# Odd attention: the loads of a head in three groups, and the next unit's maxima and shift row earlier in the unit

## The chip, the cores and the metric

The kernel runs on one core of one Trainium2 chip. The metric is the device time of one execution in microseconds (us). The core has five engines that run their own instruction lists and meet by semaphores: TensorE (PE in the profile, with its weight loads as PEld), VectorE (DVE), ScalarE (ACT), GpSimd (POOL) and SyncE (SP), which here only issues DMAs. DMAs issued by SyncE, ScalarE and GpSimd run on 16 DMA engines.

## The reference, cut to what matters

The program is a two-layer diffusion backbone (1024 latent tokens, 256 context tokens, width 1024). The second, odd, layer has a two-dimensional neighbourhood attention of 8 heads with 64 channels: the latent tokens form 16 rows of 64, each query sees 8 rows x 16 columns around it with a position bias, and all 256 context tokens besides. In short:

```python
s_loc = einsum('bchd,bicjhd->bhcij', qr, kr) * scale + bias
s_ctx = einsum('bchd,bshd->bhcs', qr, k_ctx) * scale
p = softmax(concatenate([s_loc, s_ctx], axis=-1))
o = einsum(p_loc, vr) + einsum(p_ctx, v_ctx)
```

Around it stand the even layer, a gated convolution, projections, and in each layer a mixture of 16 experts of which every token takes two. They are not touched.

## The kernel before

The program is a row of phases with a barrier of all engines at the end of each. `attend_odd` is one of them; the phases before it leave q and k (each split into a high and a low part), v and the bias tables in device memory. After it `output_odd` multiplies by the output weights.

**Units and steps.** `OddPlan` writes the order of all work into one list of events, and each engine walks through that same list and takes its own part of each event. A unit u = 2h + g is one half (g = 0 or 1, 512 queries) of head h; there are 16. A unit has 8 steps, each one block of 128 keys: two of context and six of local keys. The local ones reach only part of the 512 queries: 384, 512, 512, 512, 256, 128 columns for g = 0 and 128, 256, 512, 512, 512, 384 for g = 1. The order is context, three local, context, three local.

**One step.** `scores`: TensorE makes q times k in two products into `ps_s` (L1966 with kb and qb, L1967 with k1 and qr, whose row 64 carries minus the query's maximum, the "shift row"). For local keys VectorE adds the bias table edgeT or innerT (L1913). ScalarE takes the exponential into `pT` (L1801). `values`: TensorE multiplies by vo into `ps_o` (L1976). Scores run two steps ahead of values; `ps_s` has two buffers and `pT` three.

**Maxima and shift.** The softmax needs a maximum per query. Four `max` events of the next unit, one for each 128 queries, make q times k again, with the queries as rows (L1941 and L1942, or L1945 to L1947, into `ps_t`), and VectorE adds the table edge or inner and takes the maximum (L1889 and L1891, or L1893). After the fourth, one reduction writes minus the maxima into nmx (L1900, semaphore nmx_done). `shift`: TensorE transposes nmx in four products (L1952), and ScalarE copies the result into row 64 of qr (L1806). The first scores of a unit wait for that copy. `max` and `shift` share the two `ps_t` buffers in turn. Before the change the maxima of unit u+1 stand in steps 0 to 3 of unit u and the shift in step 6.

**The rest of a unit.** `drain`: ScalarE copies sums and totals out of `ps_o` and, after the second half of a head, issues the load of vo for head h+2 (L1818). After an odd head, VectorE inverts the sums in four reciprocals (`invert`, L1918, steps 2 to 5 of the next unit), GpSimd multiplies (L1853), ScalarE rounds the result (`normal`, L1823, step 6, ahead of the shift), GpSimd makes the low part (L1856). `weights`: in steps 3 and 7 of units 0 to 7 ScalarE rounds a piece of the output weights (L398) out of one of two buffers, GpSimd makes its low part (L1841) and issues the next load into that buffer (L1829).

**Loads.** Each head has 13 loads: qb twice and kb twice (L1778), inner twice and edge (L1769, L1770), qr (L1780), k1 (L1781), innerT twice and edgeT (L1769, L1770), all by SyncE, and vo by ScalarE. Heads h and h+2 share buffers. SyncE issues head h's loads when the last values product of head h-2 is through, and all 13 count on one semaphore, `head_in`. Three consumers wait for its full count: TensorE and VectorE at the first maximum of a head, ScalarE at the shift.

Of the kernel before, what the change touches and what calls it, by code (L numbers as in the profile page):

```python
# [31 lines left out]
P = 128  # L32
# [5 lines left out]
HD = 64  # L38
GRID_W = 64
# [78 lines left out]
def as_f32(ap):  # L118
    return ap.bitcast(F32)
# [1529 lines left out]
class OddPlan:  # L1649
# [3 lines left out]
    def __init__(self):  # L1653
        self.units = [(h, g) for h in range(8) for g in range(2)]
        self.steps, self.first, self.last = [], {}, {}
        for u, (h, g) in enumerate(self.units):
            self.first[u] = len(self.steps)
            local = self.local(g)
            self.steps += [(u, LT, 0, 4)] + local[:3] + [(u, LT + 1, 0, 4)] + local[3:]
            self.steps[self.first[u]:] = [(u, *s[1:]) for s in self.steps[self.first[u]:]]  # L1660
            self.last[u] = len(self.steps) - 1
        self.events, self.banks = [], {}
        self.next_bank, self.uses = 0, [0, 0]
        self.added, n = {}, 0
        for s, (u, kt, c0, c1) in enumerate(self.steps):
            if kt < LT:
                n += 1
            self.added[s] = n
        for j in range(4):
            self.event('max', 0, j)  # L1670
        self.event('shift', 0)
        for s in range(2):
            self.event('scores', s)
        nu = len(self.units)
        for u in range(nu):
            for s in range(self.first[u], self.last[u] + 1):
                at = s - self.first[u]
                if u + 1 < nu and at < 4:
                    self.event('max', u + 1, at)
                if u and self.units[u - 1][0] % 2:  # L1680
                    if 2 <= at < 6:
                        self.event('invert', u - 1, at - 2)
                    if at == 6:
                        self.event('normal', u - 1)
                if u + 1 < nu and at == 6:
                    self.event('shift', u + 1)
                if s % 4 == 3 and s // 4 < 16:
                    self.event('weights', s // 4)
                if s + 2 < len(self.steps):
                    self.event('scores', s + 2)  # L1690
                self.event('values', s)
            self.event('drain', u)
        for c in range(4):
            self.event('invert', nu - 1, c)
        self.event('normal', nu - 1)
# [22 lines left out]
def attend_odd(nc, k, w):  # L1718
# [2 lines left out]

    plan = OddPlan()
    units, steps = plan.units, plan.steps
    LOADS = 13
    with Phase(nc, "at1") as ph:
        kb, k1 = ([ph.sb(f"{n}{p}", [P, NT * P], F32R) for p in range(2)] for n in ("kb", "k1"))
        qb, qr = ([ph.sb(f"{n}{p}", [P, SEQ], F32R) for p in range(2)] for n in ("qb", "qr"))
# [13 lines left out]
        ps_s = [ph.ps(f"ps_s{i}", [P, 512]) for i in range(2)]  # L1741
        ps_o = [ph.ps(f"ps_o{i}", [P, 512]) for i in range(2)]
        S = {n: ph.sem(n) for n in ("filled filled_pool nmx_done shifted scored added exp_done valued drained inverted a_ready a_hi a_lo").split()}
        head_in = [ph.sem(f"head_in{p}") for p in range(2)]
        t_full = [ph.sem(f"t_full{i}") for i in range(2)]
        t_read = [ph.sem(f"t_read{i}") for i in range(2)]

# [5 lines left out]
        def emptied(eng, what, *x):  # L1753
            b, n = plan.banks[(what, *x)]
            eng.wait_ge(t_read[b], n + 1)

        def head_ready(eng, h):
            eng.wait_ge(head_in[h % 2], 16 * LOADS * (h // 2 + 1))

        with nc.Block() as block:  # L1760

            @block.sync
            def _(sp):
                def tables(h, o, edges, inners, first):

                    p = h % 2
                    for half in range(2):
                        s, a = slice(half * GRID_W, (half + 1) * GRID_W), (first + half) * GRID_W
                        sp.dma_start(inners[p][s, a:a + 8 * GRID_W], k.inner_d[o, h, s, :]).then_inc(head_in[p], 16)  # L1769
                    sp.dma_start(edges[p][:, :, :], k.edge_d[o, h]).then_inc(head_in[p], 16)  # L1770

                for h in range(8):
                    p = h % 2
                    if h >= 2:
                        sp.wait_ge(S["valued"], plan.last[2 * (h - 2) + 1] + 1)
                    r = slice(h * HD, (h + 1) * HD)
                    for dst, src in ((qb[p][0:HD, :], k.qh_d), (qb[p][HD:P, :], k.qh_d), (kb[p][0:HD, :], k.kh_d), (kb[p][HD:P, :], k.kl_d)):
                        sp.dma_start(as_f32(dst), src[r, :]).then_inc(head_in[p], 16)  # L1778
                    tables(h, 0, edge, inner, 0)
                    sp.dma_start(as_f32(qr[p][0:HD, :]), k.ql_d[r, :]).then_inc(head_in[p], 16)  # L1780
                    sp.dma_start(as_f32(k1[p][0:HD, :]), k.kh_d[r, :]).then_inc(head_in[p], 16)  # L1781
                    tables(h, 1, edgeT, innerT, 1)

            @block.scalar
            def _(act):
                for h in range(2):
                    act.dma_start(vo[h][:, :, h, :], k.v_d.rearrange("(t p) (h d) -> h p t d", p=P, d=HD)[h]).then_inc(head_in[h], 16)
                for ev in plan.events:
                    what, i = ev[0], ev[1]
                    if what == 'scores':  # L1790
# [11 lines left out]
                    elif what == 'shift':  # L1802
                        h, g = units[i]
                        ps, read = full(act, *ev)
                        head_ready(act, h)
                        nc.scalar.activation(qr[h % 2][HD:HD + 1, g * 512:(g + 1) * 512], ps[0:1, 0:512], ACT.Copy).then_inc(read, 1)  # L1806
                    elif what == 'weights':
                        w.round_hi(act, i, i + 1)
                    elif what == 'drain':
# [6 lines left out]
                        nc.scalar.activation(total[own, g, :], ps_o[g][own, :], ACT.Copy).then_inc(S["drained"], 1)  # L1816
                        if g == 1 and h + 2 < 8:
                            act.dma_start(vo[h % 2][:, :, h % 2, :], k.v_d.rearrange("(t p) (h d) -> h p t d", p=P, d=HD)[h + 2]  # L1818
                                          ).then_inc(head_in[h % 2], 16)
                    elif what == 'normal':  # L1820
                        h, g = units[i]
                        act.wait_ge(S["a_ready"], h // 2 * 2 + g + 1)
# [36 lines left out]
            def _(dve):  # L1859
# [15 lines left out]
                for ev in plan.events:  # L1875
                    what, i = ev[0], ev[1]
                    if what == 'max':
                        (h, g), j = units[i], ev[2]
                        p = h % 2
                        if j == 0:  # L1880
                            head_ready(dve, h)
                        ps, read = full(dve, *ev)
                        if i:
                            dve.wait_ge(S["nmx_done"], i)
# [16 lines left out]
                    elif what == 'scores':  # L1901
# [7 lines left out]
                        if m > 2:  # L1909
                            before = max(x for x in range(s) if plan.added[x] == m - 2 and steps[x][1] < LT)  # L1910
                            dve.wait_ge(S["exp_done"], before + 1)
                        dve.wait_ge(S["scored"], s + 1)
                        nc.vector.tensor_tensor(sb[(m - 1) % 2][:, 0:n], ps_s[s % 2][:, 0:n], tab[:, slot * GRID_W:slot * GRID_W + n], ALU.add  # L1913
                                                ).then_inc(S["added"], 1)
# [6 lines left out]
            def _(pe):  # L1921
# [8 lines left out]
                for ev in plan.events:  # L1930
                    what, i = ev[0], ev[1]
                    if what == 'max':
                        (h, g), j = units[i], ev[2]
                        p, tile = h % 2, 4 * g + j
                        if j == 0:
                            head_ready(pe, h)
                        ps, done = bank(*ev)
                        q = qb[p][:, tile * P:(tile + 1) * P]
                        ctx = kb[p][:, LT * P:NT * P]
# [14 lines left out]
                    elif what == 'scores':  # L1954
# [2 lines left out]
                        p, n = h % 2, (c1 - c0) * P  # L1957
                        if s == plan.first[u]:
                            emptied(pe, 'shift', u)
                        if s >= 2:  # L1960
                            if steps[s - 2][1] < LT:
                                pe.wait_ge(S["added"], plan.added[s - 2])
                            else:
                                pe.wait_ge(S["exp_done"], s - 1)
# [937 lines left out]
```

## Time and profile before

| what | us |
|---|---|
| median of 3 runs (lowest to highest) | 3387.43 (3386.11 to 3391.88) |
| the profiled execution | 3392.86 |
| its span in the trace | 3391.1 |
| first load of odd attention issued | 2339.0 |
| first maximum | 2361.60 |
| first scores of unit 0, of unit 15 | 2369.37, 2629.27 |
| granted TensorE clock, mean over the span | 0.868 |

Busy shares of the whole span are TensorE 76%, VectorE 46%, ScalarE 30%, GpSimd 18%. They are means over all phases; odd attention is some 300 us of the 3391. A row of a timeline has start, duration, engine, line, what is written from what, and in square brackets the idle time before it and what ended it. In the rows by stretch (rows 1) the columns are: the stretch and its length, busy time (with the number of instructions) of TensorE, its weight loads, VectorE, ScalarE and GpSimd, then the granted clock (1.00 is 2.4 GHz), the busy share of the DMA engines, and GB/s. Starts of DMA issues are marked SPq; landing times are from issue to the last byte's semaphore.

### The profile page before, as it was taken

How to read it: one execution, taken by the hardware profiler on the slowest of the kernel's cores; microseconds unless marked ns; L12 is line 12 of the kernel's file. 1: busy time of each engine (PE TensorE's matmuls, PEld its weight loads, DVE VectorE, ACT ScalarE, POOL GpSimd, SP SyncE). 2: the span in 40 equal slices, each digit the busy share in tenths (PEclk: the TensorE clock that was granted, in tenths of full speed). 3: DMA queues.
4: the chain of work that ended last, by engine and by line, in shares of the span. 5: the costliest groups of instructions: out<-in, count | busy, mean ns of one | idle time of the engine just before them, and what ended most of it. 6: DMA issues, size and time to landing. Idle time of an engine off the chain costs nothing. (4 is left out here: it accounts for less than half of the span.)

```text
span 3391.1 us, 31818 instructions
## 1 busy us (share of the span) xinstructions
PE 2580.9 (76%) x10767; PEld 1873.4 (55%) x10768; DVE 1563.3 (46%) x2166; ACT 1008.9 (30%) x1326; POOL 602.7 (18%) x560
## 2 busy tenths in 40 slices
PE   5499788898954999997337974785777792999990
PEld 0388555565633888885026532664444571788780
DVE  2255543433333566563532862333455223566754
ACT  1122242332312445442111012211433111455640
POOL 0233122111112000000121600231210332000001
PEclk9999798897966999998568987897888885999995
DMA  9111344101046777663920513666544224768856
GB/s 385 53 42 38 94 172 147 56 29 56 28 169 180 258 284 269 215 234 142 403 69 19 149 38 85 165 151 164 125 105 93 94 93 146 260 246 329 305 196 216
DMA packets 304556, 534.56 MB, mean 158 GB/s; under 512 B 126157, under 2 KB 150203, under 8 KB 298300
## 3 DMA queue, kind: packets, MB, share of 16 engines
q1 hardware_dynamic: 228848, 387.56, 34.5%
q0 software_dynamic: 25520, 85.58, 7.4%
q10 hardware_dynamic: 50076, 59.99, 5.1%
q8 instruction: 63, 1.03, 0.1%
q14 instruction: 49, 0.40, 0.0%
HBM read 431.72 MB, written 116.03 MB: 162 GB/s over the span
## 5 line engine op out<-in xcount | busy, mean ns | idle before, releaser
L2548 DVE TENSOR_TENSOR ex_gu_lo<-mw_gu,ex_gu_hi 128x2048 fp32r<-128x2048 f32 x128 | 287.3, 2287 | 78.8 <-ACT ex_gu_hi L2468 78.5
L2468 ACT ACTIVATE ex_gu_hi<-mw_gu 128x2048 fp32r<-128x2048 f32 x128 | 237.5, 1911 | 120.9 <-DVE ex_y L2595 114.8
L1611 PE MATMUL at_ps_o<-at_pT,at_v_one 128*128 128x512 f32 x336 | 187.8, 642 | 1.7 <-ACT at_pT L1391 1.7
L2626 PE MATMUL ex_ps_g<-ex_gu_hi,ex_xT_hi 128*128 128x512 f32 x408 | 169.6, 416 | 8.1 <-issue 4.9
L2626 PE MATMUL ex_ps_y<-ex_d_hi,ex_hT_hi 128*128 128x512 f32 x408 | 166.7, 409 | 9.1 <-DVE ex_d_lo L2548 7.7
L1391 ACT ACTIVATE at_pT<-at_ps_s 128x512 f32<-128x512 f32 x168 | 99.5, 595 | 232.6 <-PE at_ps_s L1604 232.3
L2548 DVE TENSOR_TENSOR ex_d_lo<-mw_d,ex_d_hi 128x2048 fp32r<-128x2048 f32 x64 | 143.8, 2288 | 53.4 <-ACT ex_d_hi L2468 53.4
L2626 PE MATMUL ex_ps_g<-ex_gu_lo,ex_xT_hi 128*128 128x512 f32 x408 | 164.7, 404 | 0.0
L2626 PE MATMUL ex_ps_g<-ex_gu_hi,ex_xT_lo 128*128 128x512 f32 x408 | 164.3, 403 | 0.0
L2626 PE MATMUL ex_ps_y<-ex_d_hi,ex_hT_lo 128*128 128x512 f32 x408 | 162.0, 397 | 0.0
L2626 PE MATMUL ex_ps_y<-ex_d_lo,ex_hT_hi 128*128 128x512 f32 x408 | 162.0, 397 | 0.0
L2626 PE MATMUL ex_ps_u<-ex_gu_hi,ex_xT_lo 128*128 128x512 f32 x408 | 161.2, 395 | 0.0
L2626 PE MATMUL ex_ps_u<-ex_gu_lo,ex_xT_hi 128*128 128x512 f32 x408 | 161.2, 395 | 0.0
L2626 PE MATMUL ex_ps_u<-ex_gu_hi,ex_xT_hi 128*128 128x512 f32 x408 | 161.2, 395 | 0.0
L2443 POOL TENSOR_TENSOR ex_at<-ex_slots,ex_nil 128x1 int32<-128x1 int32 x53 | 16.4, 310 | 804.6 <-PE ex_ps_x L2620 799.9
L1584 PE MATMUL at_ps_t<-k_both,at_q_both 128*128 128x512 f32 (+1 forms) x208 | 111.5, 576 | 54.6 <-DVE at_mx L1501 37.7
L1501 DVE TENSOR_REDUCE at_mx<-at_ps_t 128x1 f32<-128x512 f32 (+1 forms) x208 | 115.6, 582 | 46.3 <-PE at_ps_t L1584 45.0
L2468 ACT ACTIVATE ex_d_hi<-mw_d 128x2048 fp32r<-128x2048 f32 x64 | 119.1, 1908 | 28.5 <-DVE ex_y L2570 19.8
L1976 PE MATMUL at_ps_o<-at_pT,at_vo 128*128 128x512 f32 (+3 forms) x256 | 123.3, 566 | 2.9 <-ACT at_pT L1801 2.5
L865 DVE SCALAR_TENSOR_TENSOR pc_acc<-pc_yT,pc_taps,pc_acc 128x512 f32<-128x512 f32 x120 | 112.4, 1011 | 0.0
L1584 PEld LDWEIGHTS at_ps_t<-k_both,at_q_both 128*128 128x128 f32 x208 | 44.3, 213 | 116.8 <-DVE at_mx L1501 71.7
L2468 ACT ACTIVATE ex_xT_hi<-ex_ps_x 128x512 fp32r<-128x512 f32 x106 | 57.8, 596 | 171.4 <-PE ex_ps_x L2620 171.4
(486 smaller groups left out, 6130.6 us busy)
## 6 DMA issues: line engine op xcount, KB each, us to landing
mw_gu<-in_moe_w_gate SPq DMA_DIRECT2D x32, 2048.0 KB, 10.9
mw_gu<-in_moe_w_up SPq DMA_DIRECT2D x32, 2048.0 KB, 15.8
mw_d<-in_moe_w_down SPq DMA_DIRECT2D x32, 2048.0 KB, 7.7
y_d<-ex_y ACTq DMA_DIRECT2D x51, 512.0 KB
mod_mod_w<-in_ada_w SPq DMA_DIRECT2D x24, 1024.0 KB, 11.1
y_d<-at_zero POOLq DMA_DIRECT2D x36, 512.0 KB, 5.2
co_mod_w<-in_ada_w SPq DMA_DIRECT2D x16, 1024.0 KB, 14.1
edge_d<-rows_d SPq DMA_DIRECT2D x64, 160.0 KB, 3.3
```

The costliest lines, as they stand in the source:

```text
L865: ins = nc.vector.scalar_tensor_tensor(acc[q][:, c, :], src, taps[:, c, t:t + 1], acc[q][:, c, :], ALU.mult, ALU.add)
L1391: nc.scalar.activation(pT[u % 3][:, :], ps_s[u % 3][:, :], ACT.Exp).then_inc(S["exp_done"], 1)
L1501: nc.vector.tensor_reduce(mx[:, hd, c:c + 1], ps[:, :, :].rearrange("p c t -> p (c t)")[:, 0:runs[c][1]], AX.X, ALU.max).then_inc(read, 1)
L1584: nc.tensor.matmul(ps[:, :, :].rearrange("p c t -> p (c t)")[:, 0:n], q_both[i % 2][g][:, j * P:(j + 1) * P], k.k0_both[:, g, a:a + n], st ...
L1611: nc.tensor.matmul(ps_o[g][:, :], v_one[:, kt, g:g + 2, :].rearrange("p a d -> p (a d)"), pT[u % 3][:, :], start=(u == plan.first[i, g]), ...
L1976: nc.tensor.matmul(ps_o[g][:, c0 * P:c1 * P], vo[h % 2][:, kt, :, :].rearrange("p a d -> p (a d)"), pT[s % 3][:, 0:n], start=(s == plan.fi ...
L2443: nc.gpsimd.tensor_tensor(at[:, :], slots[:, bass.ds(within(n, most), 1)], nil[:, :], ALU.add).then_inc(S["at_ready"], 1)
L2468: nc.scalar.activation(dst, src, ACT.Copy).then_inc(sem, 1)
L2548: sub = lambda dst, a, b, sem: nc.vector.tensor_tensor(dst, a, as_f32(b), ALU.subtract).then_inc(sem, 1)
L2626: mm = nc.tensor.matmul(out, a[:, c, :], b[:, c, cols], start=(c == 0 and j == 0), stop=(c == chunks - 1 and j == 2))
```

## The change

The 13 loads of a head count on three semaphores: `bias_in` (3: inner twice, edge), `qk_in` (4: qb twice, kb twice) and `rest_in` (6: qr, k1, innerT twice, edgeT, vo). SyncE issues them in that order, and each group waits for what frees its own buffers in head h-2: the bias group for the last maxima, the qk and rest groups for the last scores, innerT and edgeT for the last add. VectorE's first maximum waits for `bias_in`, TensorE's for `qk_in`; the first scores product of a unit and VectorE's adds of a head's first half wait for `rest_in`; ScalarE's shift waits for no load any more. In the plan the four maxima of the next unit stand in steps 0, 0, 1 and 2, and the shift in step 4.

```diff
-                if u + 1 < nu and at < 4:
-                    self.event('max', u + 1, at)
+                for j in [j for j, turn in enumerate((0, 0, 1, 2)) if u + 1 < nu and turn == at]:
+                    self.event('max', u + 1, j)
...
-                if u + 1 < nu and at == 6:
+                if u + 1 < nu and at == 4:
                     self.event('shift', u + 1)
...
-        def head_ready(eng, h):
-            eng.wait_ge(head_in[h % 2], 16 * LOADS * (h // 2 + 1))
+        def bias_ready(eng, h):
+            eng.wait_ge(bias_in[h % 2], 16 * 3 * (h // 2 + 1))
+        def qk_ready(eng, h):
+            eng.wait_ge(qk_in[h % 2], 16 * 4 * (h // 2 + 1))
+        def rest_ready(eng, h):
+            eng.wait_ge(rest_in[h % 2], 16 * 6 * (h // 2 + 1))
...
                 for h in range(8):
                     p = h % 2
                     if h >= 2:
-                        sp.wait_ge(S["valued"], plan.last[2 * (h - 2) + 1] + 1)
+                        sp.wait_ge(S["nmx_done"], 2 * (h - 2) + 2)
+                    tables(h, 0, edge, inner, 0, bias_in)
+                    if h >= 2:
+                        sp.wait_ge(S["scored"], plan.last[2 * (h - 2) + 1] + 1)
                     r = slice(h * HD, (h + 1) * HD)
                     for dst, src in ((qb[p][0:HD, :], k.qh_d), (qb[p][HD:P, :], k.qh_d), (kb[p][0:HD, :], k.kh_d), (kb[p][HD:P, :], k.kl_d)):
-                        sp.dma_start(as_f32(dst), src[r, :]).then_inc(head_in[p], 16)
-                    tables(h, 0, edge, inner, 0)
-                    sp.dma_start(as_f32(qr[p][0:HD, :]), k.ql_d[r, :]).then_inc(head_in[p], 16)
-                    sp.dma_start(as_f32(k1[p][0:HD, :]), k.kh_d[r, :]).then_inc(head_in[p], 16)
-                    tables(h, 1, edgeT, innerT, 1)
+                        sp.dma_start(as_f32(dst), src[r, :]).then_inc(qk_in[p], 16)
+                    sp.dma_start(as_f32(qr[p][0:HD, :]), k.ql_d[r, :]).then_inc(rest_in[p], 16)
+                    sp.dma_start(as_f32(k1[p][0:HD, :]), k.kh_d[r, :]).then_inc(rest_in[p], 16)
+                    if h >= 2:
+                        sp.wait_ge(S["added"], plan.added[plan.last[2 * (h - 2) + 1]])
+                    tables(h, 1, edgeT, innerT, 1, rest_in)
...
                     elif what == 'shift':
-                        head_ready(act, h)
...
                         if j == 0:
-                            head_ready(dve, h)
+                            bias_ready(dve, h)
...
+                        if g == 0:
+                            rest_ready(dve, h)
                         dve.wait_ge(S["scored"], s + 1)
...
                         if j == 0:
-                            head_ready(pe, h)
+                            qk_ready(pe, h)
...
                         if s == plan.first[u]:
                             emptied(pe, 'shift', u)
+                            rest_ready(pe, h)
```

## Rows read from the trace of the kernel before

**Rows 1.** Busy time by stretch in odd attention (columns below).

```profile
2382.80:2393.90 11.10, 10.46 (x46) 7.21 (x46) 7.24 (x17) 6.89 (x13) 3.67 (x4) 1.00 0.14 47
2393.90:2407.00 13.10, 12.14 (x46) 7.60 (x46) 7.35 (x17) 6.92 (x13) 3.66 (x4) 1.00 0.76 157
2407.00:2418.00 11.00, 1.66 (x9) 1.32 (x9) 0.29 (x1) 2.49 (x5) 1.81 (x2) 0.68 0.90 245
2432.75:2448.50 15.75, 12.42 (x47) 7.61 (x47) 10.34 (x21) 7.77 (x14) 6.26 (x7) 1.00 0.80 164
2509.90:2527.20 17.30, 14.01 (x46) 8.54 (x46) 10.35 (x21) 7.25 (x13) 3.76 (x4) 0.89 0.72 168
```

**Rows 2.** The list of waits over odd attention: total, times, longest us.

```profile
PE at_ps_t L1941 <- DMA at_edgeT<-edge_d: 67.6, 7, 30.2
...
PE at_ps_s L1966 <- ACT at_qr L1806: 21.5, 16, 2.6
```

**Rows 3.** TensorE's timeline: first product of a unit's maxima (start, duration us).

```profile
2361.60 0.76 PE L1941 MATMUL at_ps_t<-at_kb,at_qb 128*128 128x512 f32 x1 [30.23 <-DMA at_edgeT<-edge_d]
...
2384.16 0.48 PE L1941 MATMUL at_ps_t<-at_kb,at_qb 128*128 128x512 f32 x1
...
2396.06 0.69 PE L1945 MATMUL at_ps_t<-at_kb,at_qb 128*128 128x512 f32 x1
...
2417.96 0.79 PE L1941 MATMUL at_ps_t<-at_kb,at_qb 128*128 128x512 f32 x1 [9.32 <-DMA at_edgeT<-edge_d]
...
2434.89 0.69 PE L1945 MATMUL at_ps_t<-at_kb,at_qb 128*128 128x512 f32 x1
...
2457.50 0.80 PE L1941 MATMUL at_ps_t<-at_kb,at_qb 128*128 128x512 f32 x1 [6.09 <-DMA at_edgeT<-edge_d]
...
2471.53 0.69 PE L1945 MATMUL at_ps_t<-at_kb,at_qb 128*128 128x512 f32 x1
...
2513.63 0.69 PE L1945 MATMUL at_ps_t<-at_kb,at_qb 128*128 128x512 f32 x1
```

**Rows 4.** TensorE's timeline: first scores product of units 0, 1, 4, 8, 15.

```profile
2369.37 0.79 PE L1966 MATMUL at_ps_s<-at_qb,at_kb 128*128 128x512 f32 x1 [0.67 <-ACT at_qr L1806]
...
2382.79 0.50 PE L1966 MATMUL at_ps_s<-at_qb,at_kb 128*128 128x512 f32 x1 [0.67 <-ACT at_qr L1806]
...
2432.75 0.50 PE L1966 MATMUL at_ps_s<-at_qb,at_kb 128*128 128x512 f32 x1 [2.59 <-ACT at_qr L1806]
...
2509.88 0.80 PE L1966 MATMUL at_ps_s<-at_qb,at_kb 128*128 128x512 f32 x1 [2.59 <-ACT at_qr L1806]
...
2629.27 0.50 PE L1966 MATMUL at_ps_s<-at_qb,at_kb 128*128 128x512 f32 x1 [0.67 <-ACT at_qr L1806]
```

**Rows 5.** Groups by line over odd attention.

```profile
L1893 DVE CUSTOM_DVE_ANT_0 at_junk<-at_ps_t,at_inner 128x896 f32<-128x896 f32 x32 | 34.5, 1084 | 6.8 <-PE at_ps_t L1947 6.6
...
L1918 DVE RECIPROCAL at_sums<-at_sums 128x128 f32<-128x128 f32 x32 | 29.6, 936 | 2.9 <-ACT at_total L1816 2.9
```

**Rows 6.** Timeline of one step: an add on VectorE and its values product.

```profile
2390.22 0.69 DVE L1913 TENSOR_TENSOR at_sb<-at_ps_s,at_edgeT 128x512 f32<-128x512 f32 x1
...
2391.69 1.13 PE L1976 MATMUL at_ps_o<-at_pT,at_vo 128*128 128x512 f32 x2
```

**Rows 7.** SyncE's issues, and us from issue to landing by stretch.

```profile
2342.81 0.59 SPq L1770 DMA_DIRECT2D at_edge<-edge_d  x1
...
at_edge<-edge_d SPq DMA_DIRECT2D x1, 640.0 KB, 12.5
...
ow_w_raw<-in_od_w_out POOLq DMA_DIRECT2D x2, 256.0 KB, 9.2
...
2435.37 1.08 SPq L1778 DMA_DIRECT2D at_qb<-qh_d  x2
...
2437.14 0.60 SPq L1778 DMA_DIRECT2D at_kb<-kl_d  x1
...
at_kb<-kl_d SPq DMA_DIRECT2D x1, 320.0 KB, 9.5
```

More of the change, by code:

```diff
@@ L1723, in attend_odd @@
     units, steps = plan.units, plan.steps
-    LOADS = 13
     with Phase(nc, "at1") as ph:
@@ L1743, in attend_odd @@
         S = {n: ph.sem(n) for n in ("filled filled_pool nmx_done shifted scored added exp_done valued drained inverted a_ready a_hi a_lo").split()}
-        head_in = [ph.sem(f"head_in{p}") for p in range(2)]
+        bias_in, qk_in, rest_in = ([ph.sem(f"{n}{p}") for p in range(2)] for n in ("bias_in", "qk_in", "rest_in"))
         t_full = [ph.sem(f"t_full{i}") for i in range(2)]
@@ L1763, in _, with tables @@
             def _(sp):
-                def tables(h, o, edges, inners, first):
+                def tables(h, o, edges, inners, first, sem):
                     p = h % 2
@@ L1768, in tables @@
                         s, a = slice(half * GRID_W, (half + 1) * GRID_W), (first + half) * GRID_W
-                        sp.dma_start(inners[p][s, a:a + 8 * GRID_W], k.inner_d[o, h, s, :]).then_inc(head_in[p], 16)
-                    sp.dma_start(edges[p][:, :, :], k.edge_d[o, h]).then_inc(head_in[p], 16)
+                        sp.dma_start(inners[p][s, a:a + 8 * GRID_W], k.inner_d[o, h, s, :]).then_inc(sem[p], 16)
+                    sp.dma_start(edges[p][:, :, :], k.edge_d[o, h]).then_inc(sem[p], 16)
                 for h in range(8):
@@ L1786, in _ @@
                 for h in range(2):
-                    act.dma_start(vo[h][:, :, h, :], k.v_d.rearrange("(t p) (h d) -> h p t d", p=P, d=HD)[h]).then_inc(head_in[h], 16)
+                    act.dma_start(vo[h][:, :, h, :], k.v_d.rearrange("(t p) (h d) -> h p t d", p=P, d=HD)[h]).then_inc(rest_in[h], 16)
                 for ev in plan.events:
@@ L1818, in _ @@
                             act.dma_start(vo[h % 2][:, :, h % 2, :], k.v_d.rearrange("(t p) (h d) -> h p t d", p=P, d=HD)[h + 2]
-                                          ).then_inc(head_in[h % 2], 16)
+                                          ).then_inc(rest_in[h % 2], 16)
                     elif what == 'normal':
```

## The prediction

> **What bounds the kernel now.** The kernel is one long sequence of stages with a barrier after each, and the diff touches one of them, odd attention. So I read first the busy time in stretches of that stage, then its list of waits, then TensorE's own timeline at the first product of each unit, then SyncE's issues and their landing times. The stage starts at 2339 us (the first load of head 0 at SyncE) and ends near 2640 us. A unit is half a head's queries (g is 0 or 1), eight steps long; sixteen of them follow each other, u = 2h + g.
>
> In the stretches [rows 1] TensorE is close to full between 2382.8 and 2407.0 (10.46 busy in 11.10 us, 12.14 in 13.10), at granted clock 1.00, which is 2.4 GHz. Then comes a stretch of 11.00 us with 1.66 us of TensorE's work while the DMA engines are at 0.90 and the clock falls to 0.68. The waits [rows 2] name it: seven times TensorE waits for the load into edgeT in front of L1941, 67.6 us in all. The first is the start of the stage (30.23), the other six, 37.4 us together, lie at the first maximum of heads 2 to 7 ([rows 3] has two of the six: 9.32 and 6.09). All 13 loads of a head count on one semaphore, edgeT is the last of them, and they are issued only once the last product of head h-2 is through. The second wait, 21.5 us in 16 times, is the first score product of each unit for the shift row that ScalarE copies [rows 2]. It comes in two sizes [rows 4]: 0.67 us, and 2.59 us where ScalarE's `normal` copy stands ahead of it in the same step and waits for GpSimd, which waits for the fourth reciprocal.
>
> **What a step costs.** TensorE takes a scores product of 512 columns in two matmuls and its values product in two slower ones; at 2.4 GHz I count two clocks a column for scores and four for values, 0.43 and 0.85 us (the pair of values at 2391.69 is shown with 1.13 us, its end overlapping what follows [rows 6]). With the 3328 columns of a unit, values come to 5.5 us, scores to 2.8, maxima to 1.4, transposes to 0.3: 10.0 at full clock, against 10.46 and 12.14 busy [rows 1]. VectorE: 1.1 us a maximum, 0.94 a reciprocal [rows 5], 0.69 an add of 512 columns [rows 6]. From the start of an add to the start of the values product that needs it there are 1.47 us (2390.22 to 2391.69) [rows 6].
>
> **Part 1, loads in three groups.** Nothing is removed: the same 13 loads, in another order and on three counters; SyncE has two waits more a head. What each consumer now waits for:
>
> - TensorE's first maximum waits for 4 loads (qb twice, kb twice, 1152 KB) instead of 13. They were first in the old order too, and the last of the four landed 9.5 us after its issue at 2437.14, that is 11.3 us after head 3's first issue at 2435.37 [rows 7]. They are now issued when the last scores of head h-2 are written, about 3.3 us before the next unit's first maximum (the values of three steps and the scores of two lie between: 3 x 0.85 + 0.8), and wanted one unit later. With a unit of 11 to 12.5 us (below) that is a window of 14 to 16 us against 11.3. So the whole wait goes: 37.4 us. Ahead of them in SyncE's order stand head h's bias tables, which wait for the maxima of head h-2; those are done some seven steps earlier, so this wait holds nothing up.
> - The bias tables are in flight a whole head earlier than they are wanted. The rest (qr, k1, vo, edgeT, innerT) is wanted at the first scores of the head, six steps after the first maximum: 3.3 + 11 + 8 = 22 us after the issue, against 22.1 us from first issue to release for all 13 in head 3 (2435.37 to 2457.50) [rows 3, 7]; of those 13, three (896 KB of 3840) now went earlier, so about 18. Hidden, by 4 us. Were that cover gone, TensorE would wait at the first scores.
> - At the start head 0 needs the 7 loads of bias and qk instead of 13. The seventh in the old order, edge, was issued at 2342.81 and landed 12.5 us later, at 2355.3 [rows 7]. The first maximum started at 2361.60. Gain 6.3 us. The chain from there to the first scores took 7.8 us (2361.60 to 2369.37) [rows 3, 4], so those would come at 2363.1, after the other six have landed (just before 2361.6). Bounds: 0 if the engines serve all 13 mixed, 9.5 if four loads were enough; 6.3 by the nearest row.
> - Clock. After a load wait the next unit is slower: unit 5 took 14.03 us from first maximum to first maximum (2457.50 to 2471.53), unit 1, with no wait before it, 11.90 (2384.16 to 2396.06) [rows 3]. Both have the same work. 2.13 us each, six times: 12.8 us back.
>
> **Part 2, the shift row at the fifth step.** All four maxima are sent within three steps, the shift's transposes two steps earlier. ScalarE's copy then stands before the `normal` copy, and two whole steps lie between the transposes and the product that reads the row. The 21.5 us go but for the first 0.67, which stands before the loop: 20.8 us. The long form also costs clock: in head 4's first unit 3.75 us lie between first scores and first maximum (2509.88 to 2513.63), after a wait equal in length but with the clock kept 2.14 us (2432.75 to 2434.89) [rows 3, 4]. 1.6 us, in up to five of the six places (somewhat less where the tiles are narrow): 7 us.
>
> Sum of what goes: 37.4 + 6.3 + 12.8 + 20.8 + 7 = 84.3 us.
>
> **What it adds.** TensorE runs its list in order, so the transposes now hold back all behind them until VectorE has the fourth maximum. I set out one unit, times from its first maximum on TensorE. VectorE: starts at 0.8; two maxima, an add, a maximum, an add, a maximum, the joint reduction (0.3): 0.8 + 4 x 1.1 + 1.0 to 1.3 + 0.3 = 6.5 us (odd u, whose adds are narrow) to 6.8 (even u). TensorE's own work ahead of the transposes: 5.1 in an odd unit, 6.7 in an even one. So an odd unit waits 1.4 us, an even one about none. Behind the transposes 6 products are left, some 5.2 us in an odd unit, 3.8 in an even one. Periods: 11.9 odd (as unit 1 now), 10.9 even (13.1 now in [rows 1], second row).
> Units whose predecessor ended an odd head (3, 4, 7, 8, 11, 12) have four reciprocals too. VectorE is then the longer list: 10.34 busy of 15.75 us in [rows 1]. They lie after the joint reduction in the new order, so each delays the last four adds, not the shift: chain 6.5 + 4 x 0.94 + 2 adds (1.2) + 1.47 less what overlaps, about 13.0 odd and 12.2 even, and 0.5 more in the unit after, where ScalarE's `normal` copy now stands ahead of the first exponential (0.5 x 3).
> Units 1 to 14: 4 x 11.9 + 4 x 10.9 + 3 x 13.0 + 3 x 12.2 + 1.5 = 168.3 us. Before: first scores of unit 1 at 2382.79 to those of unit 15 at 2629.27, 246.5 us [rows 4]. Saved 78.2; with 6.3 at the start and about 0.7 in unit 0: 85.2 us. The two ways of counting agree within 1 us, so the new waits are worth no more than the old small ones that also go.
> One new contention: a piece of the output weights (256 KB) takes 9.2 us to land beside the heads' loads [rows 7], and with ScalarE's 0.6, GpSimd's 1.3 and the hand-offs its loop is 11.5 us; it must fit into eight steps, which now take 10.9 to 13. ScalarE may wait up to 0.6 us in units 0 to 6: I take 2 us off in all. Taken: 83 us.
>
> The profiled execution lasted 3392.86 us (span 3391.1) and would end at 3309.9; it is 5.4 us above the median of the runs, and nothing places those 5.4 us in this stage. From the median, 3387.4 - 83 = 3304.4 us.
>
> **A rule against it.** The row first: stretches with waits of up to 0.7 us in them still have clock 1.00 [rows 1, 4]. The Trainium skill, page "TensorE: Matmul & The Clock Gate", section "A second HAM failure mode: psum-queue depth-cycling", says that frequent short idles between groups of matmuls, with PSUM banks cycled, can make the clock swing between its two levels. The new order has just such short waits, up to 1.4 us in odd units. By that rule, the rival of the clock below.
>
> **Rivals.**
> 1. As forecast, 3304 (3292 to 3317). Chance 0.66.
> 2. The order brings nothing: the transposes and the two maxima in a row hold TensorE up as long as the shift did. Only loads, start and the clock behind the loads count: 37.4 + 6.3 + 12.8 = 56.5, 3331. For it: the odd unit's 11.9 is as long as now. Against: the 2.59 us behind `normal` has a cause that the order removes. 0.13.
> 3. The four loads still come late, by 2 to 4 us, because the DMA engines are at 0.90 for most of a head's 24 us and the output weights and vo share them: with the clock 4 us x 6 = 24, 3328. The margin is 3 us by the rows. 0.10.
> 4. The clock falls in every unit: half speed for some 4 us costs 2 us a unit, 28 us in 14, 3332. 0.05.
> 5. The adds overlap better than set out; units at 10.5 to 12: 3290. 0.03.
> 6. Slower than before: the rest group comes late at the first scores of each head, because it now stands behind two waits in SyncE's order and shares the engines with the next head's tables. It has 22 us where I expect 18; it decides from 14 us late in each of six heads (18 + 4 + 14 = 36 us to land). Nothing in the rows is near that. 0.02; and 0.01 that it cancels to no change. That the diff does not do what it says I do not see: each load has its counter and each consumer a wait.
>
> **Numbers.** A change of under 0.2% (6.8 us) can't be told from none here. The range of 8 in 10 takes in cases 1 to 4: 3291 to 3333. Faster 0.97, same 0.01, slower 0.02.
>
> **What the changed profile would show.** No wait of L1941 (or L1945) for a DMA but at the start, and that one ending near 2355; the wait of the first scores for at_qr gone but once; in its place a wait of the transposes L1952 for at_nmx of about 1 us in odd units; granted clock 1.00 through the stage; units of 11 to 13 us; all later stages as long as before. It would be wrong if maxima still waited for kb, if L1967's first product of a head waited for edgeT, if the clock stayed under 1, or if VectorE's list in the units with reciprocals took over 14 us.

## The result and the profile after

The changed kernel takes 3297.29 us (median of 4 runs, 3292.36 to 3298.81), the kernel before 3388.63 (4 runs, 3386.11 to 3391.88): a ratio of 0.9727, 95% interval 0.9711 to 0.9744. That is 91.3 us less, where 83 were forecast (3304, range 3291 to 3333).

The profiled execution has a span of 3294.1 us against 3391.1. Not all of those 97 us belong to the change: the stage's first load leaves at 2330.89 us instead of 2339.01, and over all kernels here, which are the same up to that point, this start lies anywhere from 2330 to 2339. So the stage's own length is compared, from SyncE's first load for it to its first load for the next stage: 2339.01 to 2649.99 before, 311.0 us; 2330.89 to 2550.98 after, 220.1 us. The stage gives 90.9 us, the whole of the median's gain but for 0.4. Each stage length below is that of one execution, the profiled one.

Busy time by stretch after the change: the start of the stage up to the first maximum, then units 1 to 5, one a row (columns as in [rows 1]):

```profile
2330.90:2346.70 15.80, 0.01 (x1) 0.04 (x1) 4.39 (x19) 0.00 (x0) 2.40 (x4) 0.50 0.97 236
2369.00:2380.40 11.40, 11.30 (x48) 7.25 (x47) 7.28 (x18) 7.55 (x15) 3.72 (x5) 1.00 0.25 87
2380.40:2391.40 11.00, 11.00 (x49) 7.35 (x47) 7.28 (x17) 6.50 (x12) 3.62 (x4) 1.00 1.06 238
2391.40:2403.50 12.10, 11.89 (x49) 7.00 (x48) 10.33 (x22) 6.80 (x14) 4.93 (x5) 1.00 0.68 210
2403.50:2415.30 11.80, 11.35 (x47) 7.21 (x46) 10.19 (x21) 7.32 (x14) 5.83 (x6) 1.00 1.07 255
2415.30:2427.20 11.90, 11.31 (x50) 7.34 (x48) 7.42 (x18) 8.45 (x16) 5.43 (x7) 1.00 0.50 158
```

Where [rows 1] had a stretch with 1.66 us of work in 11.00 and clock 0.68, every unit now has TensorE busy for 11 us or more at clock 1.00. The list of waits of TensorE in the stage (total, times, longest), which answers to [rows 2]:

```profile
PE at_ps_t L1951 <- DMA at_kb<-kl_d: 23.4, 1, 23.4
...
PE at_ps_s L1977 <- ACT at_pT L1810: 1.8, 3, 0.6
PE at_ps_t L1962 <- DVE at_nmx L1908: 1.6, 1, 1.6
...
PE at_ps_s L1977 <- ACT at_qr L1814: 0.7, 1, 0.7
```

The wait for a DMA is there once, at the start, and the wait for the shift row once, before the loop. The wait of the transposes for nmx is there once too, before the loop; the 1 us in odd units that the prediction named among its signs did not come. TensorE's timeline at the first maximum, the first scores, and then the first maximum sent in units 1 to 5 and 14 (answers to [rows 3, 4]):

```profile
2346.69 0.77 PE L1951 MATMUL at_ps_t<-at_kb,at_qb 128*128 128x512 f32 x1 [23.44 <-DMA at_kb<-kl_d]
...
2354.47 0.79 PE L1977 MATMUL at_ps_s<-at_qb,at_kb 128*128 128x512 f32 x1 [0.67 <-ACT at_qr L1814]
...
2369.05 0.48 PE L1951 MATMUL at_ps_t<-at_kb,at_qb 128*128 128x512 f32 x1
...
2380.43 0.69 PE L1955 MATMUL at_ps_t<-at_kb,at_qb 128*128 128x512 f32 x1
...
2391.36 0.48 PE L1951 MATMUL at_ps_t<-at_kb,at_qb 128*128 128x512 f32 x1
...
2403.47 0.69 PE L1955 MATMUL at_ps_t<-at_kb,at_qb 128*128 128x512 f32 x1
...
2415.34 0.47 PE L1951 MATMUL at_ps_t<-at_kb,at_qb 128*128 128x512 f32 x1
...
2520.68 0.69 PE L1955 MATMUL at_ps_t<-at_kb,at_qb 128*128 128x512 f32 x1
```

The differences are the lengths of the units: 11.38, 10.93, 12.11, 11.87, and from there the same pattern to the end. SyncE's issues and a landing time (answers to [rows 7]): the first load of the stage, the first and the last of head 2's four qk loads, and how long the last one took:

```profile
2330.89 1.14 SPq L1774 DMA_DIRECT2D at_inner<-inner_d  x2
...
2377.74 1.25 SPq L1786 DMA_DIRECT2D at_qb<-qh_d  x2
...
2379.68 0.60 SPq L1786 DMA_DIRECT2D at_kb<-kl_d  x1
...
at_kb<-kl_d SPq DMA_DIRECT2D x1, 320.0 KB, 6.3
```

The last of the four has landed 8.2 us after the first issue (2379.68 + 6.3 - 2377.74). The product that needs it starts at 2391.36, 13.6 us after the first issue. That window is somewhat shorter than the 14 to 16 us of the prediction, since the issue came 2.7 us before the next unit's first maximum (2380.43) and not 3.3.

### The profile page after: what moved, and what is told of

The parts are those of the page before. It is cut to its first block and busy times, and to the rows that moved or that the text cites. A ratio compares the mean times of both kernels' runs of the same rounds, so it can differ in the third digit from the quotient of the medians.

```text
span 3294.1 us, 31805 instructions
## 1 busy us (share of the span) xinstructions
PE 2550.2 (77%) x10767; PEld 1851.9 (56%) x10768; DVE 1561.3 (47%) x2166; ACT 1007.5 (31%) x1326; POOL 602.1 (18%) x560
## 5 line engine op out<-in xcount | busy, mean ns | idle before, releaser
L1987 PE MATMUL at_ps_o<-at_pT,at_vo 128*128 128x512 f32 (+3 forms) x256 | 114.1, 527 | 1.2 <-ACT at_pT L1810 0.8
## 6 DMA issues: line engine op xcount, KB each, us to landing
mw_gu<-in_moe_w_gate SPq DMA_DIRECT2D x32, 2048.0 KB, 10.8
mod_mod_w<-in_ada_w SPq DMA_DIRECT2D x24, 1024.0 KB, 10.9
```

The lines of the kernel that those rows point to most:

```text
L1987: nc.tensor.matmul(ps_o[g][:, c0 * P:c1 * P], vo[h % 2][:, kt, :, :].rearrange("p a d -> p (a d)"), pT[s % 3][:, 0:n], start=(s == plan.fi ...
```

## The experiments

Stage lengths are measured as above. Each ratio is against the kernel before, run beside it on the same chip (runs 5 to 12 used another chip than runs 1 to 4); unit lengths are from first maximum to first maximum on TensorE's timeline.

| run | median us | ratio (95%) | stage us |
|---|---|---|---|
| changed kernel | 3297.3 | 0.9727 (0.9711 to 0.9744) | 220.1 |
| 1 loads alone | 3330.8 | 0.9824 (0.9799 to 0.9849) | 256.8 |
| 2 order alone | 3370.4 | 0.9940 (0.9920 to 0.9959) | 289.4 |
| 3 shift early, maxima as before | 3302.8 | 0.9750 (0.9724 to 0.9775) | 223.6 |
| 4 maxima early, shift as before | 3326.0 | 0.9812 (0.9786 to 0.9838) | 252.7 |
| 5 three counters, late issue | 3317.3 | 0.9799 (0.9780 to 0.9819) | 232.1 |
| 6 early issue, one wait | 3334.5 | 0.9845 (0.9830 to 0.9860) | 249.9 |
| 7 small reciprocals | 3295.2 | 0.9733 (0.9720 to 0.9746) | 208.5 |
| 8 shift in the sixth step | 3302.8 | 0.9749 (0.9736 to 0.9762) | 222.1 |
| 9 normal behind the scores | 3296.1 | 0.9716 (0.9701 to 0.9731) | 216.8 |
| 10 reciprocals late | 3291.6 | 0.9711 (0.9697 to 0.9724) | 211.7 |
| 11 start without vo and weights | 3308.2 | 0.9752 (0.9739 to 0.9766) | 228.2 |
| 12 both of the last two | 3306.8 | 0.9753 (0.9740 to 0.9766) | 222.5 |

### The two halves of the change: runs 1 and 2

```diff
 run 1, against the changed kernel
-                for j in [j for j, turn in enumerate((0, 0, 1, 2)) if u + 1 < nu and turn == at]:
-                    self.event('max', u + 1, j)
+                if u + 1 < nu and at < 4:
+                    self.event('max', u + 1, at)
...
-                if u + 1 < nu and at == 4:
+                if u + 1 < nu and at == 6:
```

> The loads in three groups, with maxima in steps 0 to 3 and the shift in step 6 as before. My account: load waits 37.4, start 6.3 and clock behind the waits 12.8 go, 56.5 in all, so about 3332 us; no wait of a first maximum for a DMA but at the start, and the 20.8 us of waits for the shift row stay. Rival, the order is what makes the loads arrive in time: some load waits stay and the time is over 3345.

```profile
PE at_ps_t L1951 <- DMA at_kb<-kl_d: 23.1, 1, 23.1
PE at_ps_s L1977 <- ACT at_qr L1814: 21.4, 16, 2.6
...
PE at_ps_s L1977 <- DVE at_sb L1923: 5.7, 6, 1.2
```

The median fell by 58.3 us, the stage by 54.2, for 56.5 forecast. The six load waits are gone, and the shift's waits stand at 21.4 us, as before. So the loads need nothing from the new order to arrive in time. Of the 54.2, 37.4 are load waits and 7.1 the start (15.5 us from first issue to first maximum, 22.6 before); 9.7 are left, for the clock in the main, where 12.8 were forecast. Unit 5 takes 12.88 us instead of 14.03, not 11.9. The granted clock in units 3 to 5 is still 0.92 to 0.93, with no load wait near: in units 3 and 4 it falls behind the waits for the shift row, 2.59 and 2.32 us there. So the load waits were not all that lowered the clock, and what they left over belongs to the second part of the change. The last row, waits of the scores for VectorE's adds, comes up again below.

Run 2 is the kernel before with the same two edits of the plan made the other way round.

> Maxima and shift early, all 13 loads on one semaphore as before. If the parts simply add, it gains what the loads part does not: about 35 us, 3354. My account now that both traces are read: a head's cycle is then 18 to 22 us from the last values product to the release, and one odd unit behind it. What an even unit gains comes back as a longer load wait. Only odd units 3, 7 and 11 (from 17 to 19 us down to some 14, with the slow clock at their start) and the last even one gain: about 15 us, 3373, with the load waits grown from 37 to some 55 us.

```profile
PE at_ps_t L1941 <- DMA at_edgeT<-edge_d: 85.1, 7, 33.4
...
2416.54 0.80 PE L1941 MATMUL at_ps_t<-at_kb,at_qb 128*128 128x512 f32 x1 [11.04 <-DMA at_edgeT<-edge_d]
```

Of the 85.1 us, 33.4 are the start; the six others are 51.7, against 37.4 before. The median fell by 18.7 us, the stage by 21.6. Unit 2 without its load wait got shorter by 1.4 us (12.6 to 11.2), and the wait behind it longer by 1.7 (11.04, the second row here, in place of 9.32). The two halves alone give 54.2 + 21.6 = 75.8 us of stage; together they give 90.9. The order is worth 21.6 us while the loads are late and 36.7 once they are not (256.8 to 220.1), and the difference is about what the six load waits grew by, 14.3 us. As long as loads pace a head, part of what a faster schedule gains turns into waiting for them.

### Which part of the order pays: runs 3 and 4

Run 3 has the old places of the maxima (the first edit of run 1 alone), run 4 the old place of the shift (the second alone).

> As the changed kernel, but the maxima stand in steps 0 to 3 again and only the shift is early. If the shift's place is what pays, TensorE waits up to 1 us more for the fourth maximum in some units: 3300 to 3305. Rival, sending the maxima early matters as much as the shift: 3312 or more, since the transposes then wait over 1 us in every unit.

```profile
PE at_ps_t L1962 <- DVE at_nmx L1908: 8.3, 16, 1.6
```

3.5 us of stage are lost: the transposes wait 8.3 us in 16 times for the joint reduction, where the changed kernel has 1.6 in one. Small, as expected.

> As the changed kernel, but the shift stands in step 6 again, behind ScalarE's normal copy. The waits for the shift row (0.67 and 2.6 us) come back, 20.8 us, with some of the 7 us of clock: 3318 to 3326. Rival, the early transposes cost TensorE as much as the late ones did: under 3305.

```profile
PE at_ps_s L1977 <- ACT at_qr L1814: 21.5, 16, 2.6
```

32.6 us of stage are lost (28.7 of median, the upper end of what was expected), and the shift waits are back to the tenth (21.5 in 16 times, longest 2.6). The granted clock is 0.90, 0.93 and 0.95 in units 3, 4 and 5. The early shift, ahead of the `normal` copy, carries the order's part: early maxima without it gain 4.1 us of stage over run 1, the early shift without them 33.2.

### Waiting for less, or issuing earlier: runs 5 and 6

```diff
 run 5, against the changed kernel
                     if h >= 2:
-                        sp.wait_ge(S["nmx_done"], 2 * (h - 2) + 2)
-                    tables(h, 0, edge, inner, 0, bias_in)
-                    if h >= 2:
-                        sp.wait_ge(S["scored"], plan.last[2 * (h - 2) + 1] + 1)
+                        sp.wait_ge(S["valued"], plan.last[2 * (h - 2) + 1] + 1)
...
+                    tables(h, 0, edge, inner, 0, bias_in)
...
-                    if h >= 2:
-                        sp.wait_ge(S["added"], plan.added[plan.last[2 * (h - 2) + 1]])
 run 6, against the changed kernel
                             bias_ready(dve, h)
+                            qk_ready(dve, h)
+                            rest_ready(dve, h)
...
                             qk_ready(pe, h)
+                            bias_ready(pe, h)
+                            rest_ready(pe, h)
```

> As the changed kernel, with the loads on three counters, but SyncE issues all 13 of a head when the last values product of head h-2 is through, in the old order qk, bias, rest. If issuing early is needed: kb lands 9.5 to 11.3 us after the first issue, against units of 10.9 and 11.9 us, about in time; but the edge table lands 12.5 to 16 us after it, so VectorE's first maximum is 1 to 5 us late in each of six heads, and TensorE's third maximum waits for it; with some clock lost 3310 to 3325. Rival, waiting for fewer loads is the whole of it: 3302 or less.

VectorE's wait for the bias table in run 5 (total, times, longest; the longest is the start), and TensorE's for VectorE's maxima:

```profile
DVE at_junk L1893 <- DMA at_edge<-edge_d: 25.4, 7, 9.5
...
PE at_ps_t L1951 <- DVE at_mx L1895: 10.7, 5, 2.8
```

12.0 us of stage lost, 20 us of median; the stage also starts 7.3 us later in this execution (2338.24). Units 1 to 13 alone lose 14.3 us, while the first maximum comes 3.1 us earlier, since its loads are issued ahead of the bias tables here. The wait is where it was expected: VectorE waits 15.9 us for edge in six heads, and TensorE, whose maxima fill both buffers, waits 8.6 us behind it in four heads (10.7 less 2.1 at the start). kb is in time but for 0.3 us in two heads. The run puts back the old moment and the old order of issue together, and does not tell them apart.

> As the changed kernel with its early issue, but TensorE and VectorE wait for all three counters at a head's first maximum. In the changed kernel's trace the last load of head h lands 10 to 12 us after its issue, 1 to 4 us after the first maximum that needs only kb: 15 us of waits in six heads, and some of the clock: 3312 to 3325. Rival, the early issue is the whole of it: 3302 or less.

```profile
PE at_ps_t L1955 <- DMA at_edgeT<-edge_d: 45.8, 5, 29.5
```

29.8 us of stage lost, more than the 15 to 28 expected. 16.3 us are load waits in four heads (45.8 less the start's 29.5). The slow clock behind them is some 8 us: units 1 to 13 take 176.3 us against 151.6, and the waits are 16.3 of those 24.7. The rest was left out of the expectation: the first maximum comes 21.8 us after the stage's first issue, not 15.8, since it waits for all 13 loads there too.

So neither half of the loads part does it alone: late issue in the old order costs 12 us, the joint wait 30.

### What sets the units now: runs 7 to 10

```diff
 run 7
-                        nc.vector.reciprocal(sums[:, g, c], sums[:, g, c]).then_inc(S["inverted"], 1)
+                        nc.vector.reciprocal(sums[:, g, c.start:c.start + 8], sums[:, g, c.start:c.start + 8]).then_inc(S["inverted"], 1)
 run 8
-                if u + 1 < nu and at == 4:
+                if u + 1 < nu and at == 5:
                     self.event('shift', u + 1)
```

> As the changed kernel, but each of the 32 reciprocals takes 8 of its 128 columns (the other sums are not inverted, which is part of the computation left out). If VectorE's list sets the units with reciprocals (12.1 and 11.9 us) and the one behind them (11.85), they fall to 11.4, 10.9 and 11.4: 6.5 us, and the last four, which stand alone at the end of the stage, give 2.5 to 3: about 3287 to 3289. Rival, TensorE or the order sets these units: only the last four show, 3294.

Units 3 and 4 of run 7 by stretch:

```profile
2392.40:2403.80 11.40, 11.30 (x49) 7.23 (x48) 7.67 (x22) 7.94 (x16) 5.62 (x6) 1.00 0.67 211
2403.80:2414.70 10.90, 10.90 (x49) 7.25 (x47) 7.49 (x21) 6.53 (x13) 5.61 (x6) 1.00 1.07 235
```

From unit 1 on all units are 11.39 or 10.92 us, with TensorE busy throughout. That is 11.6 us of stage less than the changed kernel: 6.4 in units 1 to 13, 3.5 behind the last maxima, where four reciprocals stand alone, and the rest at the start and in unit 0, which vary from execution to execution (in unit 0 with the moment at which the clock rises: 5.0 us into the unit in the changed kernel, 2.7 in run 9). In the median of the whole time the 8 to 10 us that were expected do not show (3295.2). The executions of this run spread over 14 us, and the profiled one was the fastest of the five (3284.5); that the reciprocals set these units rests on the lengths inside the trace. So 22.3 us a head is what TensorE's list and its short waits come to without them, and the reciprocals and the `normal` copy behind them are all that stands above it.

> As the changed kernel, but the shift stands in the sixth step instead of the fifth. If the transposes hold TensorE up in odd units (about 1 us, for the fourth maximum), a step later they don't, and one step is still enough for ScalarE's copy: 3290 to 3294. Rival, the copy then comes late for the first scores, as one step gives 1.3 us in the narrow steps of even units: 3300 or more.

```profile
PE at_ps_s L1977 <- ACT at_qr L1814: 4.5, 7, 0.9
```

Units 1 and 2 are 11.39 and 10.92, the same as with the shift a step earlier: the transposes cost nothing there. In units 3 and 4 it is worse, 13.19 and 12.53. ScalarE's copy stands there behind an exponential that waited 0.77 us for its add, an add behind a reciprocal, and TensorE waits 4.5 us in 7 times, of which one, 0.7 us, is the first. Units 1 to 13 take 155.5 us against 151.6. So the rival was right in that the copy comes late, but in the units with reciprocals, not in all even units.

```diff
 run 9: the normal event moved in the same step from ahead of 'scores' to behind it
-                    if at == 6:
-                        self.event('normal', u - 1)
...
                     self.event('scores', s + 2)
+                if at == 6 and u and self.units[u - 1][0] % 2:
+                    self.event('normal', u - 1)
 run 10
-                if u and self.units[u - 1][0] % 2:
-                    if 2 <= at < 6:
-                        self.event('invert', u - 1, at - 2)
-                    if at == 6:
-                        self.event('normal', u - 1)
+                if u > 1 and self.units[u - 2][0] % 2 and at == 1:
+                    self.event('normal', u - 2)
+                if u and self.units[u - 1][0] % 2 and at >= 4:
+                    self.event('invert', u - 1, at - 4)
...
+        self.event('normal', nu - 2)
```

> As the changed kernel, but ScalarE's normal copy stands behind the exponential of the next unit's first scores in the sixth step's list, not ahead of it. If it is this copy that makes units 5, 9 and 13 take 11.85 us against 11.38 in unit 1, they fall to 11.4: 1.4 us of the stage, 3296, too little for the whole time to tell. Rival, those 0.47 us come from VectorE's list: no change in these units.

Units 5, 9 and 13 fall from 11.85 to 11.39 us, units 3 and 4 stay at 12.11 and 11.86: the 0.46 us are the `normal` copy's. The wait of the scores for ScalarE's exponential, 1.8 us in 3 times in the changed kernel, is gone from the list. The stage is 3.3 us shorter: 1.4 here, the rest in unit 0 (11.83 against 12.93) and at the start, which vary.

> As the changed kernel, but the four reciprocals stand in steps 4 to 7 instead of 2 to 5, one a step, and the normal copy in the second step of the unit after. If the six units lose time because the reciprocals crowd the adds of steps 3 to 5, their 12.1 and 11.9 us fall to some 11.6 and 11.2, and the 11.85 behind them to 11.4: 3 to 5 us of the stage, about 3293. Rival, VectorE's whole list (10.3 busy of 12) sets them wherever they stand: no change.

Units 3 and 4 of run 10 by stretch:

```profile
2389.00:2400.40 11.40, 11.21 (x49) 7.20 (x48) 10.54 (x22) 7.81 (x15) 3.76 (x5) 1.00 0.77 230
2400.40:2411.30 10.90, 10.90 (x47) 7.25 (x46) 10.12 (x21) 7.04 (x13) 6.21 (x6) 1.00 1.07 234
```

11.39 and 10.93 us, as in run 7, but with whole reciprocals, and with VectorE busy for 10.54 of 11.40 and 10.12 of 10.90. The stage is 211.7 us, 8.4 less than in the changed kernel. VectorE's list fits into TensorE's; it was the place of the reciprocals that cost time (run 9 shows that the place of the `normal` copy leaves units 3 and 4 as they are). VectorE's rows behind the joint reduction of unit 3 show how, first the changed kernel, then run 10:

```profile
2397.33 1.75 DVE L1928 RECIPROCAL at_sums<-at_sums 128x128 f32<-128x128 f32 x2
2399.00 0.63 DVE L1923 TENSOR_TENSOR at_sb<-at_ps_s,at_edgeT 128x512 f32<-128x512 f32 x1
...
2395.03 0.69 DVE L1923 TENSOR_TENSOR at_sb<-at_ps_s,at_edgeT 128x512 f32<-128x512 f32 x1
...
2395.63 0.94 DVE L1928 RECIPROCAL at_sums<-at_sums 128x128 f32<-128x128 f32 x1
```

The second product of the scores that this add reads starts at 2396.40 in the changed kernel and at 2394.15 in run 10: the add comes 2.6 us behind it with two reciprocals ahead, 0.9 us behind it with none. Units 1 to 13 take 145.5 us against 151.6, 6.2 less where 3 to 5 were expected; the other 2.2 us of the stage are mostly its start and unit 0. This is the fastest full version, 0.9711 against 0.9727, with intervals that overlap; the order of the two rests on the stage, not on the medians.

### The start: runs 11 and 12

```diff
+                act.wait_ge(qk_in[0], 16 * 4)
                 for h in range(2):
                     act.dma_start(vo[h]...
...
-                for n in range(w.RAW):
-                    load_w(n)
                 for p in range(2):
                     nc.gpsimd.memset(vo[p][:, :, 1 - p, :], 1.0).then_inc(S["filled_pool"], 1)
+                pool.wait_ge(qk_in[0], 16 * 4)
+                for n in range(w.RAW):
+                    load_w(n)
```

> As the changed kernel, but at the start of the stage the two vo loads and the two first pieces of the output weights (1152 KB) wait until head 0's kb and qb have landed. If bytes in flight set the first maximum (15.8 us after the first issue), it comes 2 to 4 us earlier; the chain to the first scores takes 7.8 us, in which the rest must land: 2 to 4 us of the stage, 3294. Rival, the rest group is then late at the first scores and takes it back: no change.

ScalarE's issue of the two vo loads, and TensorE's first maximum and first scores:

```profile
2350.26 6.75 ACTq L1797 DMA_DIRECT2D at_vo<-v_d  x2
...
2350.38 0.77 PE L1953 MATMUL at_ps_t<-at_kb,at_qb 128*128 128x512 f32 x1 [18.81 <-DMA at_kb<-kl_d]
...
2372.19 0.76 PE L1979 MATMUL at_ps_s<-at_qb,at_kb 128*128 128x512 f32 x1 [14.71 <-DMA at_vo<-v_d]
```

The first maximum comes 11.2 us after the stage's first issue in place of 15.8, 4.6 us earlier. The first scores then wait 14.7 us for vo, which was issued at 2350.26, after most of the other loads of heads 0 and 1, and landed 22 us later; issued with the first loads it takes 11.9. The stage is 8.1 us longer, worse than the rival's no change. The load that was held back to make another one sooner is now the last that the first scores need.

> Both edits of the two runs before. If they add: 5 to 9 us less than the changed kernel, about 3290, stage 212 to 215 us against 220.1. Rival, one undoes the other through the output weights' loop: not under 217 us.

The stage is 222.5 us. Units 1 to 13 take 145.8 us, as in run 10, and the first scores wait 15.0 us for vo, as in run 11; the two edits act in different parts of the stage. The rival's number came true, by another way: not the weights, but vo.

## Why the prediction was right

**The loads.** The 37.4 us of load waits went in full, and run 1 shows that the three groups do it without the order. kb landed 8.2 us after its first issue, sooner than the 11.3 taken. vo, which left together with the first of the four before (2396.71 beside 2396.55), now leaves after the last (2381.11 after 2379.68); whether that is why was not tested apart. The start gave 6.8 us (22.6 from first issue to first maximum before, 15.8 after) for 6.3.

**The clock.** The stage runs at 1.00 from unit 1 on in every row above, and in run 8 too, with waits of up to 0.9 us. The rival of a clock that swings with short waits is refuted for this stage, and the rule it came from does not show here, that of the Trainium skill's page "TensorE: Matmul & The Clock Gate", section "A second HAM failure mode: psum-queue depth-cycling": waits of up to 0.6 us and two PSUM buffers in turn did not lower it. In run 6 load waits of 2.8 to 5.7 us brought the slow clock back, some 8 us in all. The 12.8 us of the first part were too much (9.7 at most) and the 7 of the second probably too little: run 1, without load waits, still has the lower clock behind waits of 2.3 and 2.6 us for the shift row.

**The shift row.** 20.8 us of waits went, and run 4, with the rest of the change in place, brought them back with the clock lost behind them: 32.6 us of stage. The whole order is worth 36.7 us (run 1 against the changed kernel) where the prediction's list has 20.8 + 7 = 27.8. Besides the clock, the list has no term for the scores' waits for VectorE's adds, 5.7 us in run 1 and 0.5 in the changed kernel.

**The unit set out by hand.** Units 1 to 13 (2369.05 to 2520.68) took 151.6 us; by the forecast's own figures they were 157.4. These 5.8 us, the 2 us taken off for the weights' loop and 0.5 at the start make up the 8.3 us between the 83 forecast and the 91.3 measured. (The periods of 11.9 and 10.9 are each 0.2 to 0.3 us above what the prediction's own parts add up to, 6.5 + 5.2 and 6.8 + 3.8.) The even units without reciprocals were right (10.9). Two terms were mis-sized:
- "So an odd unit waits 1.4 us." In unit 1 these are the rows around the transposes:

```profile
2373.06 0.59 PE L1987 MATMUL at_ps_o<-at_pT,at_vo 128*128 128x256 f32 x2
2373.75 0.50 PE L1977 MATMUL at_ps_s<-at_qb,at_kb 128*128 128x512 f32 x1
...
2374.48 1.12 PE L1987 MATMUL at_ps_o<-at_pT,at_vo 128*128 128x512 f32 x2
...
2374.94 0.16 DVE L1908 TENSOR_REDUCE at_nmx<-at_mx 128x4 f32<-128x8 f32 x1 [0.23 <-DVE at_mx L1901]
...
2375.44 0.60 PE L1962 MATMUL at_ps_t<-ident,at_nmx 128*128 128x128 f32 x4
```

  The transposes follow the values product at 2374.48 (0.85 us) with 0.1 us between. Ahead of them stand two waits of some 0.26 us, by my reading for an add (2373.06 with 256 columns takes 0.43, the next starts at 2373.75) and an exponential (2373.75 and 0.46, then 2374.48). So 0.6 us of waits, not 1.4, and none of them for the reduction: it was done 6.1 us after the first maximum (2369.05), not 6.5, as its maxima start 1.0 us apart and not 1.1; and TensorE's own list is some 10.8 us (11.4 less 0.6), not 10.3. The two errors partly cancel, 11.9 against 11.4. Run 8 confirms that the transposes' place is not what an odd unit is short of.
- The reciprocal units: 13.0 and 12.2 forecast, 12.1 and 11.9 measured. The chain adds up to 12.9 with nothing taken off for what overlaps, and part of the reciprocals runs while TensorE has other work: all four of 0.94 us cost 0.7 us in unit 3 (12.11 against 11.39 in run 7). The 0.5 us behind them was right (0.46, run 9).

The weights' loop made TensorE wait in no row; I did not test it apart.

**Two ways of counting.** "The two ways of counting agree" was less support than it seemed: the list of terms adds what runs 1 and 2 show not to be additive (75.8 against 90.9 us), and its parts are off in both directions (loads 56.5 against 54.2, order 27.8 against 36.7). That the two sums agreed within 1 us was in part luck.

## What to carry to other kernels

When one engine waits for the last of many loads, give each consumer a counter for what it reads, and issue each group when its own buffers are free; run 5 gives up an eighth of the stage's gain with the late issue, run 6 a third with the joint wait. Do this first, or judge a better order with care before it: in a loop paced by loads, part of its gain turns into load wait (21.6 us of stage kept of 36.7 in run 2). Then put an operation whose result starts the next unit ahead of slow side work on every engine it passes, and the side work in the steps where nobody waits for its neighbours (run 10).

## What the runs showed of the hardware that was not expected

- ScalarE's issue of two vo loads took 6.75 us from first to last when most of SyncE's loads had been issued ahead of them (run 11; 6.33 in run 12), against 1.08 us at the start of the changed kernel; what held them is not settled.
- The stage's start moved by up to 9 us between executions of kernels that are the same up to there, as much as the effects of runs 7 to 10. Units of the same work repeated to 0.02 us inside a trace and from trace to trace, with few exceptions (unit 5 of run 10 took 11.59 us, units 9 and 13 11.38 and 11.40).
